# Second mixer of a two-block transformer kernel: order of the heads, the key bias, the channel sums and the first chunk of the output projection

## The reference, cut to what matters

```python
# fox: 6 heads of 128; c = cumsum(log_f) per head
s = q @ k.T * FOX_SCALE + c[start:end, None] - c[None, :end];  p = softmax(mask(s));  y_fox = p @ v
# diff: 4 heads, two score maps of 64 each
p = softmax(mask(s1)) - lam * softmax(mask(s2));  y_diff = rmsnorm(p @ v, g_sub, 1e-5) * (1 - lam_init)
# conv: 768 channels, 31 taps
u = causal_dwconv(a * sigmoid(gt), w_dw) + b_dw;  y_conv = silu(layernorm(u, ln_g, ln_b))
y = concat([y_fox, y_diff, y_conv]) @ w_out          # 2048 x 2048
```

## Time and profile before

| | us |
|---|---|
| median of three runs | 2447.89 (2446.66 to 2450.15) |
| profiled execution, its time | 2448.83 |
| profiled execution, its span | 2447.0 |
| TensorE busy in the span | 2329.1 (95%) |
| VectorE, ScalarE busy | 1523.3, 1048.3 |
| last product of `w_in_2` starts / first product of chunk 0 of the output projection starts | 1480.33 / 1562.78 |
| first product of chunk 1 starts | 1594.65 |

### The profile page before, as it was taken

The page is one execution under the profiler, slowest core; times in us unless marked ns, Lnnn a source line. Parts: engine busy times, 40 slices in busy tenths (PEclk is TensorE's granted clock), DMA queues, the critical chain, the costliest instruction groups (busy, mean ns, idle before and its releaser), DMA issues.

```text
span 2447.0 us, 41728 instructions
## 1 busy us (share of the span) xinstructions
PE 2329.1 (95%) x16374; PEld 2169.4 (89%) x16374; DVE 1523.3 (62%) x1718; ACT 1048.3 (43%) x1225; POOL 123.0 (5%) x248
## 2 busy tenths in 40 slices
PE   3999989899999999999899999898999999999997
PEld 3899768899998899988799996698999978999986
DVE  7988689654554476644644995546665644566545
ACT  5463243544443344343544434445444433344333
POOL 0000023000001100001100000000000011000010
PEclk9999989999999999999999998799999999999999
DMA  9988859555555588745455551154555555555552
GB/s 394 422 328 332 320 204 388 165 189 184 183 183 193 185 282 285 274 169 192 140 175 171 173 179 60 51 174 138 190 177 187 187 188 189 189 189 173 189 187 103
DMA packets 162958, 506.49 MB, mean 207 GB/s; under 512 B 8096, under 2 KB 12496, under 8 KB 134048
## 3 DMA queue, kind: packets, MB, share of 16 engines
q1 hardware_dynamic: 161536, 500.28, 58.2%
q0 software_dynamic: 752, 3.48, 0.5%
q10 hardware_dynamic: 576, 1.44, 0.2%
HBM read 503.07 MB, written 2.10 MB: 206 GB/s over the span
## 4 chain that ended last, share of the span: by engine, by line
PE 88%; DVE 5%; DMA 4%; ACT 2%; issue 1%; SPq 0%; ACTq 0%; DVEq 0%
PE pb L560 23%; PE pb L547 18%; PE pb L548 18%; PE pb L549 18%; DMA raw<-w_in 3%; PE pb L526 1%; PE pb L528 1%; PE pb L527 1%; PE pb L676 1%; PE pb L910 1%; DVE x L1605 1%; PE pb L1112 1%; DVE wlo L489 1%; DMA raw<-w_ada 1%; DVE raw L454 1%
## 5 line engine op out<-in xcount | busy, mean ns | idle before, releaser
L443 DVE TENSOR_TENSOR wlo<-raw,whi 128x1024 fp32r<-128x1024 f32 (+1 forms) x712 | 862.7, 1221 | 745.4 <-ACT whi L436 744.1
L436 ACT ACTIVATE whi<-raw 128x1024 fp32r<-128x1024 f32 (+1 forms) x712 | 746.0, 1054 | 1082.6 <-PE pb L549 715.0
L547 PE MATMUL pb<-xh,whi 128*128 128x256 f32 (+2 forms) x3760 | 1063.5, 283 | 5.2 <-DVE xl L1791 2.5
L548 PE MATMUL pb<-xl,whi 128*128 128x256 f32 (+2 forms) x3760 | 1063.1, 283 | 0.0
L549 PE MATMUL pb<-xh,wlo 128*128 128x256 f32 (+2 forms) x3760 | 1061.9, 282 | 0.0
L547 PEld LDWEIGHTS pb<-xh,whi 128*128 128x128 f32 x3760 | 710.5, 189 | 6.7 <-DVE xl L1791 2.8
L548 PEld LDWEIGHTS pb<-xl,whi 128*128 128x128 f32 x3760 | 710.4, 189 | 0.0
L549 PEld LDWEIGHTS pb<-xh,wlo 128*128 128x128 f32 x3760 | 710.2, 189 | 0.0
L560 PE MATMUL pb<-whi,stg 128*128 128x512 f32 x1664 | 451.2, 392 | 15.3 <-DVE hb L1638 5.1
L560 PEld LDWEIGHTS pb<-whi,stg 128*128 128x128 f32 x1664 | 314.4, 189 | 85.1 <-issue 6.8
L560 PE MATMUL pb<-wlo,stg 128*128 128x512 f32 x832 | 258.4, 392 | 0.0
(11 more groups left out here) (368 smaller groups left out, 1618.2 us busy)
## 6 DMA issues: line engine op xcount, KB each, us to landing
raw<-w_ada SPq DMA_DIRECT2D x79, 1024.0 KB, 7.0
raw<-w_ffn_gate SPq DMA_DIRECT2D x44, 1024.0 KB, 5.2
raw<-w_ffn_up SPq DMA_DIRECT2D x44, 1024.0 KB, 5.2
raw<-w_ffn_down SPq DMA_DIRECT2D x44, 1024.0 KB, 4.7
raw<-w_gate SPq DMA_DIRECT2D x44, 1024.0 KB, 5.2
raw<-w_up SPq DMA_DIRECT2D x44, 1024.0 KB, 5.2
raw<-w_down SPq DMA_DIRECT2D x44, 1024.0 KB, 4.8
raw<-w_in SPq DMA_DIRECT2D x40, 1024.0 KB, 5.0
```

The lines of the kernel that those rows point to most:

```text
L436: act.activation(to, src, ACT.Copy).then_inc(hi_ready, 1)
L443: dve.tensor_tensor(to, src, hi, ALU.subtract).then_inc(raw_done, 1)
L547: mm(o, whi[:, s, t], xh[:, k, c0:c1], start=(k == 0), stop=False)
L548: mm(o, whi[:, s, t], xl[:, k, c0:c1], start=False, stop=False)
```

## The change

- **Heads.** TensorE does `scores(0)` ahead of the steps, and step s does `scores(s+1)`, `pv(s-2)`, `turn(s-1)`. VectorE does `maxima(0)` ahead, and step s does `maxima(s+1)`, `probs(s)`, `rest(s-2)`.
- **Key bias.** `cfn` is split into an fp32r part and its remainder, rows 0-5 and 32-37 of `cfr`; `pick` holds ones at both; one fp32r product of 38 rows replaces the fp32 product of 6 rows.
- **Channel sums.** VectorE sums the 6 tiles (`channel_sum`, one TENSOR_REDUCE with a strided read), TensorE multiplies only the sum by ones.
- **Front.** 5 idle fp32 products ahead of the transposes of v; the copy to `vM` in two parts; ScalarE copies the last `w_in_2` chunk out of PSUM ahead of the split of half 3 of `w_out_2`.
- **Chunk 0 of `w_out_2`.** The rows of y and `w_out_2` are in the order fox, conv, diff (`w_out_rows` permutes the weight's rows on their way in). Half 0 goes behind `turn(8)`, halves 1 and 2 behind the last `pv`, 3 and 4 behind the conv part, then `pe_turn_yd`, half 5, and 6 and 7 behind the diff part. Halves 4 to 7 are split within the mixer.
- **Norm of the diff heads** in two parts of two heads (`yd_clip`, `yd_squares`, `yd_sums`), the first while head 9 is still under way.

```diff
 def pe_mixer2():
+        pe.wait_ge(bank_free, BF_WIN2 + 10)
+        pe_idle(5, 7)
         pe.wait_ge(bank_free, BF_WIN2 + 11)
...
                     if h < FH:
-                        last = mm(o, kc[0:FH, K_ID + h:K_ID + h + 1].to_broadcast([FH, m]), cfn[:, 0:nk], start=False,
+                        last = mm(o, pick[0:BIAS_K, h:h + 1].to_broadcast([BIAS_K, m]), cfr[0:BIAS_K, 0:nk], start=False,
                                   stop=True)
...
-            for c in range(CT6):
-                last = mm(pb[:, bank, 0:NQ], ones, zT2[:, tile + c, 0:NQ], start=(c == 0), stop=(c == CT6 - 1))
-            last.then_inc(done, 1)
+            mm(pb[:, bank, 0:NQ], ones, zT2[:, CH_SUM, 0:NQ], start=True, stop=True).then_inc(done, 1)
...
+        scores(0)
         for s in range(HEADS2 + 2):
-            if s < HEADS2:
-                scores(s)
+            if s + 1 < HEADS2:
+                scores(s + 1)
+            if s >= 2:
+                pv(s - 2)
             if 1 <= s <= HEADS2:
                 turn(s - 1)
-            if s >= 2:
-                pv(s - 2)
             if s == 0:
-                pe.wait_ge(sem("conv"), TAPS * CT6)
-                over_channels(1, 2, sem("ln_mean"))
+                pe.wait_ge(sem("conv"), TAPS * CT6 + 1)
+                over_channels(1, sem("ln_mean"))
             if s == 2:
-                pe.wait_ge(sem("ln_sq"), 1)
-                over_channels(3, 8, sem("ln_var"))
+                pe.wait_ge(sem("conv"), TAPS * CT6 + 2)
+                over_channels(3, sem("ln_var"))
+            if s == HEADS2 - 1:
+                pe.wait_ge(sem("max2"), HEADS2)
+                pe.wait_ge(sem("o2_out"), FH)
+                out2_half(0)
+        out2_half(1)
+        out2_half(2)
+        pe.wait_ge(sem("mix2"), 1)
+        out2_half(3)
+        out2_half(4)
+        pe_turn_yd()
+        out2_half(5)
+        mix2_over(pe)
+        for h in (6, 7):
+            out2_half(h)
 act_mixer2():
+            if s == HEADS2:
+                act.wait_ge(sem("ln_y"), CT6)
+                act.activation(zT2[:, 2:8, 0:NQ], zT2[:, 8:14, 0:NQ], ACT.Sigmoid).then_inc(sem("ln_sig"), 1)
+                yd_squares(0)
             if 1 <= s <= HEADS2:
                 pT_out(s - 1)
...
+        weights_hi(4)
+        act.wait_ge(sem("ln_out"), 1)
+        act.activation(xh[:, Y_CONV, 0:NQ], zT2[:, 8:14, 0:NQ], ACT.Copy).then_inc(sem("mix2_hi"), 1)
+        yd_squares(1)
+        weights_hi(5)
         act.wait_ge(sem("yd_ms"), 1)
         act.activation(ydst[:, 4, :], ydst[:, 2, :], ACT.Sqrt).then_inc(sem("yd_rt"), 1)
+        weights_hi(6)
+        weights_hi(7)
 dve_forget():
-        dve.tensor_scalar(cfn[:, :], cfn[:, :], -float(HD) ** 0.5, None, ALU.mult).then_inc(sem("cf_done"), 1)
+        dve_link(dve.tensor_scalar(cfn[:, :], cfn[:, :], -float(HD) ** 0.5, None, ALU.mult))
+        dve_link(dve.tensor_scalar(cfr[0:BIAS_K, :], kc[0:BIAS_K, 0:T2], 0.0, None, ALU.mult))
+        dve_link(dve.tensor_copy(cfr[0:FH, :], cfn[:, :]))
+        dve.tensor_tensor(pick[0:BIAS_K, 0:FH], kc[0:BIAS_K, K_ID:K_ID + FH], kc[0:BIAS_K, K_ID + LO_AT:K_ID + BIAS_K], ALU.add)
+        dve.tensor_tensor(cfr[LO_AT:BIAS_K, :], cfn[:, :], cfr[0:FH, :].bitcast(F32), ALU.subtract).then_inc(sem("cf_done"), 1)
 dve_mixer2():
+        dve.wait_ge(sem("conv"), TAPS * CT6)
+        channel_sum(2)
+        maxima(0)
         for s in range(HEADS2 + 2):
+            if s + 1 < HEADS2:
+                maxima(s + 1)
             if s < HEADS2:
-                maxima(s)
                 probs(s)
             if s >= 2:
                 rest(s - 2)
             layer_norm(s)
+            if s == HEADS2 - 1:
+                yd_clip(0)
+            if s == HEADS2:
+                dve.wait_ge(sem("ln_sig"), 1)
+                dve.tensor_tensor(cy, cy, ch, ALU.mult).then_inc(sem("ln_out"), 1)
+                yd_sums(0, 0)
+                yd_sums(0, 1)
+        yd_clip(1)
+        dve.wait_ge(sem("mix2_hi"), 1)
+        dve.wait_ge(sem("ln_out"), 1)
+        dve.tensor_tensor(xl[:, Y_CONV, 0:NQ], cy, xh[:, Y_CONV, 0:NQ].bitcast(F32), ALU.subtract).then_inc(sem("mix2"), 1)
+        yd_sums(1, 0)
...
+        yd_sums(1, 1)
+        weights_lo(4)
...
         dve.tensor_tensor(v, sc, sm, ALU.add).then_inc(sem("yd_ms"), 1)
+        weights_lo(5)
...
+        weights_lo(6)
+        weights_lo(7)
+        dve.wait_ge(sem("mix2_hi"), 2)
```

More of the change, by code:

```diff
@@ L256, in meta_columns, with w_out_rows @@
     return np.ascontiguousarray(np.concatenate([tokens, g.reshape(KT, P).T], axis=1))
+def w_out_rows(w):
+    fox, diff, conv = np.split(w, (FOX_W, FOX_W + DIFF_W), axis=1)
+    return np.ascontiguousarray(np.concatenate([fox, conv, diff], axis=1))
 def w_in_units(w):
@@ L531, in w_in_chunk, with chunk_half @@
                 behind[h]()
+    def chunk_half(h, u, w, b0, c0, c1, at=in_row, n0=0, nf=4, width=CW, i=0, nu=0):
+        s = (w + h) % SLOTS
+        pe.wait_ge(raw_done, 2 * (u + at(n0 + h // 2)) + h % 2 + 1 + i * (2 * nu))
+        for kk in range(2):
+            k = 2 * h + kk
+            for f in range(nf):
+                o = pb[:, b0 + f, 0:c1 - c0]
+                t = slice(kk * width + f * P, kk * width + (f + 1) * P)
+                mm(o, whi[:, s, t], xh[:, k, c0:c1], start=(k == 0), stop=False)
+                mm(o, whi[:, s, t], xl[:, k, c0:c1], start=False, stop=False)
+                last = mm(o, wlo[:, s, t], xh[:, k, c0:c1], start=False, stop=(k == KT - 1))
+        last.then_inc(used, 1)
     def chunk(u, w, b0, c0, c1, at=in_row, n0=0, nf=4, width=CW, i=0, nu=0, x_split=None,
@@ L537, in chunk @@
         for h in range(8):
-            s = (w + h) % SLOTS
-            pe.wait_ge(raw_done, 2 * (u + at(n0 + h // 2)) + h % 2 + 1 + i * (2 * nu))
             if x_split is not None and h % 2 == 0:
                 pe.wait_ge(sem("x_split"), x_split + h // 2 + 1)
[L542 to L550, removed]
+            chunk_half(h, u, w, b0, c0, c1, at, n0, nf, width, i, nu)
             if behind is not None and h in behind:
@@ L1119, in turn @@
             if h == 0:
[L1120 removed]
+                pe.wait_ge(sem("v2_out"), 4)
             pe.wait_ge(sem("probs2"), h + 1)
@@ L2074, in meta_sum @@
                 .then_inc(sem("meta_ss"), 1)
-        pe.wait_ge(sem("o2_out"), HEADS2)
-        for c in range(4):
+        for c in range(1, 4):
             at_least(pe, sem("oT_out"), c - 1)
@@ L2080, in _ @@
                 rows_read(c - 1)
-            chunk(U_WOUT2 + 4 * c, W_WOUT2 + 8 * c, 4 * (c % 2), 0, NQ,
-                  behind={FH // 2 - 1: pe_turn_yd, 4: lambda: mix2_over(pe)} if c == 0 else {3: lambda: turn_o(c - 1)})
+            chunk(U_WOUT2 + 4 * c, W_WOUT2 + 8 * c, 4 * (c % 2), 0, NQ, behind={3: lambda: turn_o(c - 1)})
         turn_o(3)
@@ L2241, in _ @@
         for c in range(4):
-            for h in range(8 * c + 4, 8 * c + 12):
+            for h in range(8 * c + 4 + 4 * (c == 0), 8 * c + 12):
                 if h < 2 * KT:
@@ L2402, in meta_scale @@
             dve_link(dve.tensor_tensor(m_row, m_row, m_rt_all, ALU.mult))
-        for h in range(4, 2 * KT):
+        for h in range(8, 2 * KT):
             split_lo(U_WOUT2 + h // 2, W_WOUT2 + h, h % 2)
```

79 lines of the change are left out of this document (49 added, 30 removed).

## The result

The changed kernel takes 2429.97 us (median of four, 2427.55 to 2433.76) against 2448.01 (four, 2446.66 to 2450.15): ratio 0.9919, 95% interval 0.9905 to 0.9933. That is 18.0 us less where 25.5 were forecast; the time lies inside the range of 2414 to 2434, 7.6 above its point. The profiled execution took 2429.20, with a span of 2427.4 and a mean clock of 0.982 (0.977 before).

What follows compares the result with a forecast made beforehand. TensorE bounds: its own work in fox heads, idle and clock in diff heads. 31.5 us saved at 2.4 GHz, less 4 for clock and 2.0 for forget gate, is 25.5: 2447.9 to 2422.4 us, range 2414 to 2434.

Steps and rivals of the forecast that it cites:

- What bounds it: Whole kernel: 88% of the chain is TensorE, so time comes only from its idling, low clock or removable work.
- Mixer at full clock less 4 for two stretches: Last w_in_2 product to chunk 1: 31.5 us saved at 2.4 GHz, less 4 for two stretches at 1.2 GHz.
- the charge for the clock: Mixer: 4 us charged for two stretches of some 3 to 7 us at 1.2 GHz, beside gaps of about 1 us.
- Channel sum on VectorE: Each reduction of 1,548 elements takes 1.75 us, bound 3.5; TensorE waits 0.6 for the second.
- Forget gate: Four more VectorE operations ahead of a split in w_in_2: gap 0.82 becomes 2.1; cost 2.0 us, bounds 1.0 and 3.0.
- Bias: Fox heads: the new key bias product costs 0.30 us a head instead of 1.22; a head takes 3.75.
- Front: Transposes of v start at 1482.8, run 0.11 us apart at 2.4 GHz; scores start at 1486.9 instead of 1489.2.
- Diff heads, norm, chunk 0: Diff heads need 5.1 us of TensorE work each; half 3 doesn't wait, the serial norm and 2.54 us waits are covered.
- Serial heads: Rival, chance 0.12: diff heads stay at 6.5 us instead of 4.9, gain only 19 us, 2429.
- Dear bias: Rival, chance 0.08: the fp32r bias product isn't cheaper, up to 5.5 us less gain, 2428.
- The clock stays low in the diff heads: Rival, chance 0.17: the old share of 1.2 GHz persists, costing 14 instead of 4 us; gain 15.5, 2432.
- Slower: Rival, chance 0.03: halves and heads all run at 1.2 GHz with denser interleaving of small products; 2463 us.

Runs made afterwards that it cites:

- after_again: The changed kernel rerun with no edit, for a closer ratio and a second profile: 2429.85 us, ratio 0.9911 to the kernel before.
- forget_later: Changed kernel with VectorE's forget gate part moved behind the first row of taps: 2427.05 us, ratio 0.9904 to the kernel before.
- no_idle: Changed kernel without the 5 idle products ahead of the transposes of v: 2425.98 us, ratio 0.9898 to the kernel before.
- two_fill: Changed kernel with forget gate later, channel sums as three additions, four idle products ahead of each of pv(7) and pv(9): 2421.64 us.
- half_behind: Changed kernel with half 0 of chunk 0 behind all heads instead of behind turn(8): 2433.94 us, ratio 0.9934 to the kernel before.
- sums_pairwise: Changed kernel with each channel sum as three unit-stride additions instead of one strided reduction: 2423.32 us, ratio 0.9891 to the kernel before.
- bias_fp32: Changed kernel with the old 6-row fp32 bias product and without the four VectorE operations for its split: 2435.03 us.
- heads_old: Changed kernel with the old order of the heads on TensorE and VectorE: 2442.56 us, ratio 0.9962 to the kernel before.

## Why the prediction was right, and where it was off

**What bounds it: right.** Idle time, clock and removable work were the three places, and 7.1, 13.8 and 6.3 us came out of them. The channel sums gave 4.2 instead of the 4.6 forecast, since two instructions cost 0.64 from row to row and not 0.47.

**Mixer at full clock less 4 for two stretches: right in the first profile.** 27.5 were forecast, 27.2 came. The losses were two stretches of 6.8 us, at `pv(7)` and `pv(9)`, for which waits of about 1 us had been named; they measured 0.83. The named wait for probs(8) is hidden in this profile behind the slowed `pv(7)` (no wait ahead of the turn at 1539.38); after_again, forget_later and no_idle have it, at 1.15 to 1.16. Full clock itself was right too: two_fill, which never runs at 1.2 GHz in the mixer but adds the channels pairwise, takes 81.9 us from the last `w_in_2` product to chunk 1, where 82.8 was forecast.

**The step that was mis-sized is the charge for the clock.** The 4 us hold for the first profile. after_again, the same kernel, has 23.9 us at 1.2 GHz instead of 13.7 and takes 4.5 us more, and forget_later, no_idle and half_behind, with the same channel sums, have 23.9 too. Two terms stand behind it, one that was taken below its size and one whose second part was only named:

- *Channel sum on VectorE*: 1.75 taken, with 3.5 as the bound for a strided read; 2.8 measured. The wait for the second sum, 0.6 in the prediction, became 1.01, and behind it the clock usually fell for 13.7 us. sums_pairwise takes it away and returns 6.4 from B to C, 6.5 in the medians.
- *Forget gate*: 2.0 taken. The wait grew by 1.41 where 1.25 had been reckoned (gap 2.1 forecast, 2.23 found), and with it came the fall of the clock that had been held possible: 2.9 altogether in the usual execution, just under the upper bound of 3.0. forget_later and bias_fp32 show it.

Together: 25.5 - 4.5 - 0.9 = 20.1, against 18.0 and 20.9 in the two comparisons. That is the missing part, as far as single profiles stand for the median; that the sum lands between the two is partly luck, since one and the same kernel gave 97.2 and 101.7.

**Bias: mis-sized, made up elsewhere.** 0.30 a head was taken. From row to row a bias of 272 columns costs 0.31 (1495.44 to 1495.75), one of 144 costs 0.26 (1494.52 to 1494.78), one of 16 costs 0.10: 0.67 in all. About half of the old price was saved and not three quarters, 2.2 us less over six heads. A head costs 4.1 (turns at 1500.62 and 1504.73), not 3.75. But this longer work filled most of the idle time forecast ahead of the first turn, 1.9 us, of which 0.36 was left, and the front was 1.0 us early; by turn 5 gains and losses cancel (35.6 us behind the last `w_in_2` product forecast, 35.8 found). That they do so nearly was luck.

**Front: right, and 1 us better.** Scores start 5.6 us behind the last `w_in_2` product instead of the 6.6 forecast, since ten idle instructions last 1.27 and not 2.1, and the last `w_in_2` chunk is out of PSUM when they end. The transposes ran 0.11 apart, as said, so the Trainium skill's rule that they don't count as busy for the clock ("TensorE: Matmul & The Clock Gate", Part 4) would have made them slower than the trace has them. no_idle shows that the reason given, idle products keep the clock up, isn't what did it.

**Diff heads, norm, chunk 0: right.** Turns of the diff heads lie 4.9 to 5.5 apart until half 0, and no wait stands ahead of halves 3 or 6 or of chunk 1, as forecast.

**The rivals.** *Serial heads* is refuted: the diff turns lie 4.9 to 5.5 us apart, and 6.8 in heads_old, where the heads are serial. *Dear bias* came true in part, 2.2 of its 5.5 us. *The clock stays low in the diff heads* did not come as put; the falls that cost most were in the fox heads, behind one wait. *Slower* had nothing for it: the clock stood higher than before, 0.92 against 0.79 over the stretch.

## What to carry to other kernels

Price a wait on TensorE by what the clock does behind it: here 1 us of waiting cost 6.4 against a profile in which the clock fell and 1.9 against one in which it did not, and the same instructions gave 97 or 102 us in two executions, so take more than one profile before a loss or a gain of some us is put down to an edit. Issue the next unit's first stage ahead of the present one's later stages where the other engines' passes stand between: that was worth 13.5 of 20.9 us here, most of it through the clock and 2.7 as waits. When work moves from a bounding engine to another, ask whether the receiving side gets it in an order it reads well, and whether the place it gets was already one that the bounding engine waited for.

## What the hardware did that had not been expected

- A TENSOR_REDUCE that reads six tiles with a stride took 2.79 to 2.84 us for 1,548 elements; three adds with unit stride took 0.97 + 0.43 + 0.43. One of these adds took 1.20 in the first sum and 0.43 in the second, at the same shape. The slow one ran beside a GpSimd copy (from 1491.21, 1.44 us, against 1.09 in the changed kernel), the fast one beside none, in all four kernels with the adds; whether that is the cause was not tried.
- An fp32r product of 38 rows cost 0.31 us at 272 columns and 0.26 at 144, more than twice the 0.12 of a 128-row one in a run of like products. It stands between fp32 products on other data; which of the two makes it dear was not tried.
- The clock fell with TensorE busy without a gap (bias_fp32), fell or stayed behind the same wait of 1.0 us in two executions of the same kernel, and stayed through a gap of 1.17 (no_idle).
